# Two attention heads side by side on TensorE, and masked biases built by DMA, in a two-layer decoder trunk

## The reference, cut to what matters

```python
DIL_PAIRS = ((128, 1), (512, 4), (2048, 16))          # window, dilation of the 3 query groups
scores = einsum(q, k) * 64 ** -0.5                    # per head, 256 x 256, causal
scores = where(allowed[group], scores + bias[rel_bucket(distance), head], NEG_INF)
m_g, l_g, o_g = max, sum(exp(scores - m_g)), exp(scores - m_g) @ v
out = sum_g(exp(m_g - m) * o_g) / sum_g(exp(m_g - m) * l_g)      # layer 0: one softmax over the 3 groups
logits = einsum(q_lat, c_sel) * 64 ** -0.5 + bias                # layer 1: only the picked keys
cross  = softmax(q @ k_mem * 64 ** -0.5) @ v_mem                 # both layers, 4 heads
```

## Time and profile before

| what | us |
|---|---|
| runs, median (lowest to highest of 3) | 1661.31 (1659.61 to 1663.27) |
| profiled execution, its own time | 1662.92 |
| profiled execution, span from the first to the last instruction | 1661.1 |
| busy in the span: TensorE, VectorE, ScalarE, GpSimd | 1584.7, 1306.5, 1117.8, 79.8 |
| attention stream of layer 0, from its first scores to its last mixing | 62.6 to 265.9 |
| attention stream of layer 1, the same | 529.5 to 648.4 |

### The profile page before, as it was taken

One profiled execution on the slowest core, in us unless ns is written; L12 is line 12 of the kernel. 1 busy time (PEld: TensorE's weight loads), 2 busy tenths in 40 slices (PEclk: granted clock), 3 DMA queues, 4 the chain that ended last, 5 costly groups with the idle time before them and its releaser, 6 DMA issues.

```text
span 1661.1 us, 25537 instructions
## 1 busy us (share of the span) xinstructions
PE 1584.7 (95%) x8450; PEld 1341.2 (81%) x8450; DVE 1306.5 (79%) x1687; ACT 1117.8 (67%) x1442; POOL 79.8 (5%) x57
## 2 busy tenths in 40 slices
PE   7899988999988989799999999999999999999996
PEld 6899966999987766688888888888888888888885
DVE  4777755555557763799899899899899899999996
ACT  5554445434443653687887878888878878878874
POOL 1422100000000000000000000000000000000000
PEclk9999988999998998799999999999999999999998
DMA  9744425566632235599999999999999999999992
GB/s 263 196 126 119 135 64 149 158 187 181 186 84 66 81 129 189 182 401 387 367 398 386 356 389 382 374 385 376 382 384 367 390 383 367 391 385 354 403 387 77
DMA packets 226976, 455.34 MB, mean 274 GB/s; under 512 B 12832, under 2 KB 120496, under 8 KB 226928
## 3 DMA queue, kind: packets, MB, share of 16 engines
q1 hardware_dynamic: 222784, 439.52, 72.9%
q0 software_dynamic: 4144, 15.22, 3.7%
HBM read 445.52 MB, written 9.18 MB: 274 GB/s over the span
## 4 chain that ended last, share of the span: by engine, by line
PE 90%; DVE 5%; ACT 2%; DMA 2%; issue 1%; DVEq 0%; POOL 0%; ACTq 0%; POOLq 0%
PE ps L664 27%; PE ps L665 26%; PE ps L666 26%; PE ps L737 2%; DMA big<-in_even_w_in 2%; PE ps L1029 1%; DVE w_lo L1345 1%; PE ps L759 1%; PE ps L735 1%; PE ps L746 1%; ACT w_hi L1065 1%; PE ps L691 1%; PE ps L763 0%; PE ps L971 0%; PE ps L962 0%
## 5 line engine op out<-in xcount | busy, mean ns | idle before, releaser
L1345 DVE TENSOR_TENSOR w_lo<-big,w_hi 128x1024 fp32r<-128x1024 f32 (+1 forms) x843 | 992.4, 1218 | 233.8 <-ACT w_hi L1065 157.0
L1286 ACT CAST w_hi<-big 128x1024 fp32r<-128x1024 f32 x672 | 693.8, 1056 | 138.0 <-PE ps L666 134.0
L664 PE MATMUL ps<-w_hi,m_hi 128*128 128x512 f32 (+1 forms) x1008 | 393.7, 391 | 4.6 <-DVE w_lo L1345 4.6
L665 PE MATMUL ps<-w_lo,m_hi 128*128 128x512 f32 (+1 forms) x1008 | 391.0, 388 | 0.0
L666 PE MATMUL ps<-w_hi,m_lo 128*128 128x512 f32 (+1 forms) x1008 | 390.6, 388 | 0.0
L664 PE MATMUL ps<-h_hi,w_hi 128*128 128x256 f32 (+1 forms) x824 | 240.5, 292 | 5.0 <-DVE w_lo L1345 5.0
L665 PE MATMUL ps<-h_lo,w_hi 128*128 128x256 f32 (+1 forms) x824 | 236.2, 287 | 0.0
L666 PE MATMUL ps<-h_hi,w_lo 128*128 128x256 f32 (+1 forms) x824 | 235.9, 286 | 0.0
L1065 ACT CAST w_hi<-big 128x1024 fp32r<-128x1024 f32 (+1 forms) x171 | 165.3, 977 | 95.5 <-PE ps L666 82.7
L664 PEld LDWEIGHTS ps<-w_hi,m_hi 128*128 128x128 f32 x1008 | 190.6, 189 | 44.7 <-issue 7.2
L666 PEld LDWEIGHTS ps<-w_hi,m_lo 128*128 128x128 f32 x1008 | 190.6, 189 | 38.7
(11 more groups left out here) (218 smaller groups left out, 1320.4 us busy)
## 6 DMA issues: line engine op xcount, KB each, us to landing
big<-in_odd_w_gate SPq DMA_DIRECT2D x112, 1024.0 KB, 7.3
big<-in_odd_w_up SPq DMA_DIRECT2D x112, 1024.0 KB, 7.5
big<-in_odd_w_down SPq DMA_DIRECT2D x112, 1024.0 KB, 7.4
big<-in_even_w_in SPq DMA_DIRECT2D x42, 512.0 KB, 4.2
big<-in_even_w_gate SPq DMA_DIRECT2D x22, 512.0 KB, 3.9
big<-in_even_w_up SPq DMA_DIRECT2D x22, 512.0 KB, 3.8
big<-in_even_w_down SPq DMA_DIRECT2D x22, 512.0 KB, 3.5
big<-in_w_out SPq DMA_DIRECT2D x20, 512.0 KB, 4.4
```

Of the source, the lines that this page charges most:

```text
L664: mm(dst, a[0], b[0], start=start, stop=False, **kw)
L665: mm(dst, a[0], b[1], start=False, stop=False, **kw)
L1286: nc.scalar.copy(w_hi[:, slot, :], ring[s][:, (u % 2) * UNIT:(u % 2 + 1) * UNIT]).then_inc(s_hi, 1)
L1345: return V.tensor_tensor(dst, src, lead.bitcast(F32), ALU.subtract)
```

## The change

- **Scores.** `scores(pair)` makes both heads' scores together. It issues their matmuls in turn, head 0 on partitions 0 to 63 and head 1 on 64 to 127, never into the same PSUM bank at one time. In layer 0 the third group of both heads' second tiles goes to the bank that the k projection has left (`third_left` and `third_read` guard it).
- **Mixing.** `mix(pair)` does both heads together, in turn, head 0 into partitions 0 to 63 and head 1 into 64 to 127 of bank 6. Each head has its own `probs`, its own transposed `probs_turned`, and its own `z` (head 1 takes the place of the indexer's tiles `qiT` and `kiT`, now one tile `zq`).
- **Order.** Each `step` is written anew: TensorE now does `p(0)`, values, `p(1)`, turn head 0, `p(2, 3)`, turn head 1, scores of `nxt`, `p(4)`, mix. `head_scores(pair)` reads both heads; in layer 0 it reads the third group of both first.
- **Biases.** GpSimd adds the masks once, to the rows of 16 heads, before they go to DRAM (8 copies of three masked rows a head, and 8 of the plain rows). For each pair of layer 0, 16 transfers of 8 partitions, 6 rows of 1 KB each, bring the masked biases into `bmp` with the skew. `bias` comes by 16 such transfers behind the first two pairs. The three 128 x 256 masks are no longer loaded.

```diff
-COPIES = 32
+COPIES = 8
@@ gpsimd
+            pool.dma_start(drows, consts[0:HEADS, C_DROWS:C_DROWS + NBR * 384].rearrange("h (b j) -> h b j", b=NBR)).then_inc(s_dr, 16)
+            pool.dma_start(con[:, C_CAUSAL:C_HOT], consts[:, C_CAUSAL:C_HOT]).then_inc(s_con, 16)
             pool.wait_ge(s_eb, 1)
+            pool.wait_ge(s_dr, 16)
+            nc.gpsimd.tensor_tensor(ebuf[:, 0:NBR, :], drows, ebuf[:, NBR:NBR + 1, :].broadcast_to([HEADS, NBR, 384]),
+                                    ALU.add).then_inc(s_em, 1)
+            pool.wait_ge(s_em, 1)
             pool.wait_ge(s_x[TT - 1], 16)
+            src = ebuf[:, 0:NBR, :].rearrange("h (o b) j -> h o (b j)", o=1).broadcast_to([HEADS, COPIES, NBR * 384])
+            pool.dma_start(scratch_m.rearrange("p h j -> h p j"), src).then_inc(s_mrow, 16)
...
+            def masked(g):
+                if g >= 2:
+                    pool.wait_ge(s_at[0]["scores_read"], 2 * g - 1)
+                for p0 in range(0, P, COPIES):
+                    skew = bass.AP(scratch_m.tensor, P - 1 - p0 + 2 * g * WIDTH,
+                                   [[HEADS * WIDTH - 1, COPIES], [384, 2 * NBR], [1, 256]])
+                    dst = bmp[p0:p0 + COPIES, g % 2, :, :, :].rearrange("p h b s -> p (h b) s")
+                    pool.dma_start(dst, skew).then_inc(s_bm[g % 2], 16)
+            masked(0)
+            masked(1)
             pool.wait_ge(s_scrw, 16)
             for p0 in range(0, P, COPIES):
                 ...  # bias, as before
+            for g in range(2, PAIRS):
+                masked(g)
-            (mask_pair and its loop)
@@ tensor
+            def scores(pair):
...
+                if pair.nbr == 1:
+                    turns = [[(0, 0), (1, 0)]] * 2
+                else:
+                    turns = [[(1, 2), (0, 0), (0, 1), (0, 2), (1, 0), (1, 1)], [(1, 0), (0, 0), (0, 1), (0, 2), (1, 1), (1, 2)]]
+                for i in range(len(turns[0])):
+                    for hh in range(2):
+                        t, b = turns[hh][i]
+                        r = slice(HD * hh, HD * hh + HD)
+                        last = mm(score_columns(pair, hh, t, b, b + 1)[:, 0, :], qT[r, pair.par, b, tok(t)],
+                                  k[r, 0:SEQ if pair.cross or t else P], start=True, stop=True)
+            def mix(pair):
...
+                for t in range(TT):
+                    for hh in range(2):
+                        h = slice(HD * hh, HD * hh + HD)
+                        n0 = 0 if pair.cross else P * t
+                        last = mm(ps[h, 6, n0:SEQ], v[:, t, h], probs_turned(pair, hh)[:, SEQ * t:SEQ * (t + 1) - n0],
+                                  start=(t == 0), stop=(t == TT - 1))
@@ tensor, step
+                p(0)
                 if not now.cross:
                     turn_values(now)
+                p(1)
                 turn_probs(now, 0)
+                p(2, 3)
+                turn_probs(now, 1)
                 if nxt is not None:
+                    scores(nxt)
                 p(4)
+                mix(now)
@@ scalar, step (layer 1 and cross: the second branch)
                 exps(now, 0)
                 if now.kind == "even":
                     e(0)
+                    values()
                     hi_mat(aft, 0)
                     e(1)
+                    exps(now, 1)
                     hi_mat(aft, 1)
                     probsT(now, 0)
                     e(2)
                     hi_mat(aft, 2)
                     e(3)
+                    probsT(now, 1)
                     hi_mat(aft, 3)
                     e(4)
                     hi_mat(aft, 4)
                 else:
                     exps(now, 1)
                     e(0)
+                    values()
                     outs(hi, now, 0)
                     probsT(now, 0)
+                    hi_mat(aft, 0)
                     e(1)
                     e(2)
+                    probsT(now, 1)
+                    outs(hi, now, 1)
                     hi_mat(aft, 1)
                     hi_mat(aft, 2)
                     outs(hi, now, 2)
@@ vector
+            def head_scores(pair):
+                if pair.kind == "even":
+                    dve.wait_ge(s_bm[pair.par], 16 * (P // COPIES) * pair.idx + 16 * (P // COPIES))
+                    dve.wait_ge(S["scores"], 2 * pair.g + 2)
+                    read_scores(pair, 0, 1, 2, 3)
+                    read_scores(pair, 1, 1, 2, 3).then_inc(S["third_read"], 1)
+                for hh in range(2):
...
+                    read_scores(pair, hh, 0, 0, pair.nbr)
+                    read_scores(pair, hh, 1, 0, min(pair.nbr, 2)).then_inc(S["scores_read"], 1)
...  (mask and maxima of this head, as before)
             def step(now, nxt, aft):
+                head_probs(now, 0)
                 if now.kind == "even":
                     lo_mat(aft, 0)
                     lo_mat(aft, 1)
                     head_probs(now, 1)
+                    lo_mat(aft, 2)
+                    lo_mat(aft, 3)
                 else:
+                    head_probs(now, 1)
+                    outs(lo, now, 0)
                     lo_mat(aft, 0)
...
                 if nxt is not None:
+                    head_scores(nxt)
+                if now.kind == "even":
+                    lo_mat(aft, 4)
```

More of the change, by code:

```diff
@@ L707, in project @@
                     pe.wait_ge(S["evacuated"], n - 1)
+                if pair.l == 0 and m == 0 and norm is None:
+                    pe.wait_ge(S["third_read"], PAIRS if pair.cross else pair.g)
                 src, kc = (CS, RC) if pair.kind == "odd" and m > 0 else (HS, DC)
@@ L717, in turn_values @@
                 for t in range(TT):
-                    last = tr(ps[:, 7, tok(t)], vT[:, tok(t)], ident)
+                    last = tr(value_bank(pair)[:, tok(t)], vT[:, tok(t)], ident)
                 last.then_inc(S["turned_v"], 1)
@@ L742, in turn_probs @@
                 pe.wait_ge(S["probs"], 2 * pair.g + hh + 1)
-                pe.wait_ge(S["probsT"], 2 * pair.g + hh + 1)
+                pe.wait_ge(S["probsT"], 2 * pair.g + 1 + (hh if pair.kind == "even" else 0))
+                if pair.kind == "even" and not hh:
+                    pe.wait_ge(S["values"], pair.g + 1)
                 for a, b in ([(0, 0), (1, 2), (2, 1), (3, 3)] if pair.cross else [(0, 0), (1, 1), (2, 2)]):
-                    last = tr(ps[:, 5, tok(b)], pn[:, tok(a)], ident)
+                    last = tr(turned(pair, hh)[:, tok(b)], probs(pair, hh)[:, tok(a)], ident)
@@ L829, in stream @@
                     pe.wait_ge(s_me, 2 * 2)
-                scores(first, 0)
+                scores(first)
                 steps(l, pe, step)
@@ L1116, in exps @@
                 act.wait_ge(S["max"], 2 * pair.g + hh + 1)
+                if pair.kind == "even" and hh:
+                    act.wait_ge(S["summed"], 2 * pair.g + 1)
                 zv, pv, n0 = views(pair, hh)
@@ L1124, in probsT @@
                 act.wait_ge(S["probs_turned"], 2 * pair.g + hh + 2)
-                act.wait_ge(S["mixed"], 2 * pair.g + hh + 1)
+                act.wait_ge(S["mixed"], 2 * pair.g + 1)
                 n = 512 if pair.cross else CAUSAL
-                nc.scalar.copy(pts[:, 0:n], ps[:, 5, 0:n]).then_inc(S["probsT"], 1)
+                nc.scalar.copy(probs_turned(pair, hh)[:, 0:n], turned(pair, hh)[:, 0:n]).then_inc(S["probsT"], 1)
             def step(now, nxt, aft):
@@ L1134, in e, with values @@
                         evac(nxt, m)
-                if not now.cross:
-                    act.wait_ge(S["turned_v"], now.g + 1)
-                    nc.scalar.copy(vN[:, :, :].rearrange("p t n -> p (t n)"), ps[:, 7, 0:SEQ]).then_inc(S["values"], 1)
+                def values():
+                    if not now.cross:
+                        act.wait_ge(S["turned_v"], now.g + 1)
+                        nc.scalar.copy(vN[:, :, :].rearrange("p t n -> p (t n)"), value_bank(now)).then_inc(S["values"], 1)
                 exps(now, 0)
@@ L1148, in step @@
                     e(3)
+                    probsT(now, 1)
                     hi_mat(aft, 3)
-                    probsT(now, 1)
                     e(4)
@@ L1204, in _ @@
             mem_out(1)
-            act.wait_ge(s_scrw, 16)
             stream(0, 3)
@@ new lines, in read_scores @@
+            def read_scores(pair, hh, t, b0, b1):
+                zv, pv, n0 = views(pair, hh)
+                dst = zv[:, b0:b1, (0, n0)[t]:(n0, n0 + SEQ)[t]]
+                src = score_columns(pair, hh, t, b0, b1)
+                if pair.cross:
+                    return V.tensor_scalar(dst, src, SCALE, None, ALU.mult)
+                cols = slice(P, SEQ) if t == 0 else slice(0, SEQ)
+                add = bmp[:, pair.par, hh, b0:b1, cols] if pair.l == 0 else bias[:, bass.ds(2 * pair.g + hh, 1), cols]
+                return V.scalar_tensor_tensor(out=dst, in0=src, scalar=SCALE, in1=add, op0=ALU.mult, op1=ALU.add)
```

201 lines of the change are left out of this document (78 added, 123 removed).

## The result

The changed kernel takes 1638.43 us (median of 4 runs, 1637.07 to 1639.46), and the kernel before 1660.46 in the same comparison: a ratio of 0.987, 95% interval 0.9845 to 0.9894. The forecast was 1617, and its range ended at 1638. The profiled execution took 1638.63 us with a span of 1636.8.

What follows compares the result with a forecast made beforehand. TensorE was taken to bound layer 0's steps, latency the tails. Gains of 19.4 + 9 + 7 + 11 = 46.4 us from 1662.9 gave 1616.5, 1615 against the median, set to 1617 for omissions; range 1608 to 1625.

Steps and rivals of the forecast that it cites:

- Start: Layer 0's first weights: up to 4 us gained at 44 us, up to 4 lost by 65; taken as 0.
- Biases: 16 new transfers a pair in layer 0, taken at 0.65 us issue each; hidden up to 1.18 us a transfer.
- The slower rival: Small transfers come late, VectorE waits at a pair's first read and TensorE with it; 1836 us, chance 0.08.
- A step of layer 0: One attention step in layer 0 takes 19.0 us instead of 21.65; 19.4 us gained over the layer's steps.
- The column halves: Rival: in mixing, the column halves don't overlap, costing 0.5 us a layer 0 step; 1626 us, chance 0.17.
- the one of binding chains: VectorE's and ScalarE's chains bind more; steps of 20.3 us in layer 0, 9.4 in layer 1; 1636 us, chance 0.13.
- Layer 1: Layer 1's steps: ScalarE's chain bounds at 8.7 us against 9.6; 7 us gained for seven steps (0 to 10).
- Tails: From the last pair's scores on: 9 us gained in layer 0 (6 to 12), 11 in layer 1 (8 to 14).
- no 4 us wait in the tails: Sign that the forecast holds: TensorE no longer stands still about 4 us at the end of each layer's attention.
- GpSimd's additions: Mask additions in layer 0's steps, hidden themselves; without their disturbance VectorE gains 1 us and more a step.
- Sum: All gains in both layers' attention: 19.4 + 9 + 7 + 11 = 46.4 us.

## Why the prediction came out wrong

- **Start** is the step that failed: "up to 4 us gained at 44 us and up to 4 lost by 65. I take 0". It measured +26.9 us. The gain at 44 us was there (layer 0's first unit is rounded 9.7 us earlier), but its fifth and sixth come at 64.1 and 79.8 us, where they came at 50.4 and 52.2. I had moved 2 MB in the queue without asking what the 16 transfers do to the engines that the weights need at the same time: only their order was weighed, and their bytes, not their time on the engines. The trace of before has transfers to 32 neighbouring partitions alone; for those to 8 no row gave a time, and I took 0.
- **Biases**, in the running steps: right. "I take the issue, 0.65": it is 0.555 us, a landing takes 5.2 us in the middle and 12.5 at most, and no engine waits for them. The estimate that I had worked out from the Trainium skill, DMA: Bandwidth & Descriptors, rules for kernel authors, 32 us a pair if the small transfers went in a row, did not come: they don't go in a row, with issues 0.56 us apart and landings of 5.2. But the DMA share of a step is 0.93, not the 0.42 of before plus a little, and 0.68 with partitions 4 apart: the steady state had room for the slowness, the start had none.
- **The slower rival** was near the cause ("8 partitions reach fewer DMA engines than 32, perhaps") and had it in the wrong place: I priced it for the bias's own readers, and it hit the weights, which share the engines. What counts is how many groups of destination partitions a transfer reaches, as the table shows, and not that it has 8; whether fewer engines also take part was not separated.
- **A step of layer 0**: forecast 19.0 us, measured 18.8 to 18.9 (19.5 the first). TensorE busy 18.69 of 18.87: it bounds, and VectorE's 15.08 is under the 16 that I had summed. The whole: -21.0 where 19.4 was forecast. The column halves overlap, so that rival is out; so is the one of binding chains.
- **Layer 1**: step 8.62 for 8.7, with TensorE busy 7.36 only, so the chain through VectorE and ScalarE bounds as argued (the chain that ended last in this window has 6.5% on its largest TensorE piece). The whole: -9.0 for 7. About 6 of it is the six later steps (9.6 us before); the other 3 is the first step, 11.6 us before and 8.6 now, which I had not counted by itself.
- **Tails**: -8.0 for 9, and -12.6 for 11. The sign "no 4 us wait in the tails" did not come: TensorE's longest wait there, for `pr` before a transpose, is 3.4 us in layer 0 and 4.2 us in layer 1 (waits, 588.9 to 625.1 us: total, times, longest):

```profile
PE ps L793 <- DVE pr L1471: 5.1, 3, 4.2
```

- **GpSimd's additions** were counted for their effect on VectorE, "1 us and more a step": 1.7 on VectorE, 1.1 in the step.
- **Sum**: 50.6 for 46.4 without the start, 4.2 too few. The changed kernel with `bias` late ran at 1615.6, which is near 1617 only because its start still cost 3 us.

Still open: why 8 partitions 16 apart cost more of q0 than 16 neighbours with as many groups (132 against 111 us a MB); and whether the engines' number takes part.

## What to carry to other kernels

Price an added transfer by the time it takes on the DMA engines that others share, not by its bytes or its queue, and look for the stretch where those engines already are the bound: here the stretch from 26 to 80 us, where 48 such transfers cost 27 us, while 96 more of their kind in the steps cost nothing. If a transfer must be of few partitions (8 here), let them lie 4 apart and not side by side. And issue what is wanted late (layer 1's bias) late.

## What was not expected of the hardware

- Skewed transfers of 8 neighbouring partitions held the engines 167 us a MB, against 80 with as many partitions 4 apart, and a second queue's full-width weights paid alike (179 against 87).
- TensorE overlaps two heads' passes that are issued one head after the other wholly for 4 passes each (8 in 0.60 us), and only in part for 12 (3.4 us against 2.2).
- GpSimd `tensor_tensor` instructions of 1.9 us nearly double VectorE's two-input additions beside them (540 to 895 ns, 558 to 1047).
